# Attention of an encoder layer: scores three units ahead, a fourth slot of probabilities, one weighing run for a pair of units

## What is computed

```python
logits = jnp.einsum('bqkgd,bjkd->bkgqj', q_blk, k_blk) * scale + bias
logits = jnp.where(valid, logits, -jnp.inf)
m = jnp.maximum(jnp.max(logits, axis=-1), sink_f)
p = jnp.exp(logits - m[..., None])
denom = jnp.sum(p, axis=-1) + jnp.exp(sink_f - m)
probs = p / denom[..., None]
out = jnp.einsum('bkgqj,bjkd->bqkgd', probs, v_blk)
...
mix = jnp.concatenate([rms_norm(attn, g_attn), rms_norm(four, g_four)], axis=-1) @ w_o
x = layer_norm(ALPHA * x + mix, ln1_g, ln1_b)
```

## Time and profile before

| | |
|---|---|
| median of three runs (lowest, highest) | 962.12 us (962.06, 963.3) |
| the profiled execution: its own time, its span | 963.37 us, 961.6 us |
| busy, share of the span: TensorE, VectorE, ScalarE, GpSimd | 98%, 82%, 49%, 29% |
| attention stage in the trace | about 153 to 222 us |

### The profile page before, as it was taken

The page is one execution under the profiler, slowest core; times in us unless marked ns, Lnnn a source line. Parts: engine busy times, 40 slices in busy tenths (PEclk is TensorE's granted clock), DMA queues, the critical chain, the costliest instruction groups (busy, mean ns, idle before and its releaser), DMA issues.

```text
span 961.6 us, 12084 instructions
## 1 busy us (share of the span) xinstructions
PE 944.0 (98%) x4402; PEld 773.6 (80%) x4402; DVE 786.2 (82%) x1147; ACT 471.7 (49%) x706; POOL 282.2 (29%) x257
## 2 busy tenths in 40 slices
PE   7999999999999999999999999999999999999996
PEld 6888887667888788888888888888888888888885
DVE  5666488987886899889798888898888699977798
ACT  5575467868014664554455445445545754333200
POOL 2300327993940000010010001100000199990032
PEclk9999999999999999999999999999999999999999
DMA  8245153928031136365555464654527886564212
GB/s 312 83 87 175 22 132 136 304 45 305 10 144 43 67 91 160 79 164 132 121 142 134 100 172 100 142 148 105 153 66 262 339 340 232 190 229 171 96 66 109
DMA packets 110811, 142.06 MB, mean 148 GB/s; under 512 B 21164, under 2 KB 72320, under 8 KB 110753
## 3 DMA queue, kind: packets, MB, share of 16 engines
q1 hardware_dynamic: 104352, 129.69, 40.6%
q0 software_dynamic: 5184, 9.44, 7.2%
q10 hardware_dynamic: 1216, 2.17, 0.7%
HBM read 112.18 MB, written 47.97 MB: 167 GB/s over the span
## 4 chain that ended last, share of the span: by engine, by line
PE 93%; DVE 4%; issue 2%; DMA 1%; ACT 0%; POOL 0%; SPq 0%; DVEq 0%
PE ps L792 28%; PE ps L794 28%; PE ps L793 28%; PE ps L1042 2%; PE ps L1021 2%; DVE bn L1301 1%; DVE acc L1862 1%; PE ps L998 1%; PE ps L1154 1%; PE ps L999 1%; DMA acc<-in_x_prompt 1%; PE ps L827 1%; DVE pT L1518 0%; DVE prob L1510 0%; DVE mv L1305 0%
## 5 line engine op out<-in xcount | busy, mean ns | idle before, releaser
L792 PE MATMUL ps<-db_hi,ga_hi 128*128 128x512 f32 x252 | 98.0, 389 | 0.0
L793 PE MATMUL ps<-db_lo,ga_hi 128*128 128x512 f32 x252 | 98.0, 389 | 0.0
L794 PE MATMUL ps<-db_hi,ga_lo 128*128 128x512 f32 x252 | 98.0, 389 | 0.0
L792 PE MATMUL ps<-x1h,wa_hi 128*128 128x512 f32 x192 | 75.6, 394 | 0.0
L794 PE MATMUL ps<-x1h,w_lo 128*128 128x512 f32 x192 | 74.8, 389 | 0.0
L2220 ACT ACTIVATE hc<-U,taps 128x512 f32<-128x512 f32 x60 | 48.7, 813 | 53.1 <-DVE U L1697 41.5
L793 PE MATMUL ps<-x1l,wa_hi 128*128 128x512 f32 x192 | 74.7, 389 | 0.0
L737 POOL TENSOR_TENSOR acc<-acc,gain_bc 128x1024 f32<-128x1024 f32 x12 | 40.5, 3374 | 84.6 <-ACT bias_bc L1912 84.6
L2225 ACT ACTIVATE hc<-hc 128x512 f32<-128x512 f32 x44 | 27.9, 633 | 71.3 <-DVE hc L1714 71.3
L1912 ACT ACTIVATE ga_hi<-ga_raw 128x1536 fp32r<-128x1536 f32 x21 | 31.3, 1490 | 62.0 <-DMA db_raw<-in_w_down 28.8
L1298 DVE TENSOR_TENSOR ga_lo<-ga_raw,ga_hi 128x1536 fp32r<-128x1536 f32 x21 | 48.5, 2310 | 9.9 <-ACT ga_hi L1912 9.9
(11 more groups left out here) (314 smaller groups left out, 2892.5 us busy)
## 6 DMA issues: line engine op xcount, KB each, us to landing
w_raw<-in_w_up SPq DMA_DIRECT2D x44, 512.0 KB, 4.9
ga_raw<-gs_scratch SPq DMA_DIRECT2D x21, 768.0 KB, 4.6
ts_scratch<-in_w_down SPq DMA_DIRECT2D x12, 768.0 KB, 14.9
gs_scratch<-gsum SPq DMA_DIRECT2D x9, 1024.0 KB, 4.5
db_raw<-ts_scratch SPq DMA_DIRECT2D x12, 768.0 KB, 6.2
db_raw<-in_w_down SPq DMA_DIRECT2D x9, 768.0 KB, 6.5
ts_scratch<-in_w_down POOLq DMA_DIRECT2D x18, 256.0 KB, 5.1
gs_scratch<-gated SPq DMA_DIRECT2D x9, 512.0 KB
```

What stands on the lines that cost most here:

```text
L792: pe.matmul(out, whi, xhi, start=start, stop=False, skip_group_check=onto)
L793: pe.matmul(out, whi, xlo, start=False, stop=False, skip_group_check=onto)
L794: return pe.matmul(out, wlo, xhi, start=False, stop=stop, skip_group_check=onto)
```

## The change

A fourth slot of probabilities is added (`prob3`, for which the values of the second sequence move to another place), and `negm`, `rowsum` and `rden` get a fourth entry. TensorE's loop has a step more: step `m` has the scores of unit `m + 2` and the turns of unit `m - 1`. The weighing of a pair is one run of all key blocks, every second step. The second half of the last projection, `project(11, 1)`, stands among the scores of the first step, and the third run of `out_four` ahead of the last turns. On VectorE the two copies of a unit stand directly behind the four `logits`, and `attn_low` and `wo_low` behind them; ScalarE's loop follows the same steps. GpSimd's order stays, with four slots instead of three. No engine computes anything more or less.

```diff
-    negm = keep("negm", [P, 3, GRP])
+    negm = keep("negm", [P, 4, GRP])
...
-    vz1 = at("vz1", [P, TB, P], F32, 134912)
+    vz1 = at("vz1", [P, TB, P], F32, 184064)
...
     prob = at("prob", [P, 3, GRP, 3 * P + 1], F32, 8192)
+    prob3 = at("prob3", [P, GRP, 3 * P + 1], F32, 130816)
+    probs = [prob[:, 0], prob[:, 1], prob[:, 2], prob3[:]]
...
-            def weigh_pair(e, blocks):
+            def weigh_pair(e):
...
-                elif blocks[0] == 0:
+                else:
                     pe.wait_ge(o_sq, e - 1)
                     pe.wait_ge(o_lo, e - 1)
-                for i in blocks:
+                for i in range(len(kbs)):
...
-                if blocks[-1] == len(kbs) - 1:
-                    last.then_inc(pv_done, 1)
+                last.then_inc(pv_done, 1)
...
-            for n in range(UNITS):
-                if n == 1:
-                    project(11, 1)
-                if n >= UNITS - 2:
-                    out_four(n - UNITS + 2)
+            for m in range(UNITS + 1):
+                n = m - 1
+                if m >= UNITS - 2:
+                    out_four(m - UNITS + 2)
                 for j in range(GRP):
-                    if n + 2 < UNITS:
-                        scores(n + 2, j)
-                    if 1 <= j <= len(key_blocks(unit(n)[0])):
+                    if m + 2 < UNITS:
+                        scores(m + 2, j)
+                    if m == 0 and j == 2:
+                        project(11, 1)
+                    if m and 1 <= j <= len(key_blocks(unit(n)[0])):
                         turn_probs(n, j - 1)
-                if n >= 2:
-                    blocks = range(len(key_blocks(PAIRS[n // 2 - 1][0])))
-                    weigh_pair(n // 2 - 1, blocks[-1:] if n % 2 else blocks[:-1])
-            weigh_pair(UNITS // 2 - 1, range(2))
-            out_four(2)
+                if n >= 2 and n % 2 == 0:
+                    weigh_pair(n // 2 - 1)
+            weigh_pair(UNITS // 2 - 1)
             out_attn(0)
...
-                if n >= 3 and j == 0:
-                    dve.wait_ge(pt_ps, pt_before(n - 2))
+                if n >= 4 and j == 0:
+                    dve.wait_ge(pt_ps, pt_before(n - 3))
...
-            for n in range(UNITS):
-                for j in range(GRP):
-                    if n + 2 < UNITS and j < 2:
-                        logits(n + 2, j)
-                    if n == 1 and j == 1:
-                        proj_low(11)
-                    if n + 2 < UNITS and j == 1:
-                        logits(n + 2, 2)
-                        logits(n + 2, 3)
-                    if j == 1 and n >= 5 and n % 2:
-                        attn_low((n - 5) // 2)
-                    if j == 1 and n - 1 in WO_UNITS:
-                        wo_low(0, WO_UNITS.index(n - 1))
-                    if 1 <= j <= 2:
-                        probs_out(n, j - 1)
+            for m in range(UNITS + 1):
+                n = m - 1
+                if m + 2 < UNITS:
+                    for j in range(GRP):
+                        logits(m + 2, j)
+                if m == 0:
+                    proj_low(11)
+                    continue
+                for i in range(2):
+                    probs_out(n, i)
+                if n >= 5 and n % 2:
+                    attn_low((n - 5) // 2)
+                if m - 1 in WO_UNITS:
+                    wo_low(0, WO_UNITS.index(m - 1))
                 if n == UNITS - 1:
                     for k in range(4):
                         wo_low(1, k)
                     attn_low(UNITS // 2 - 2)
```

More of the change, by code:

```diff
@@ L210, in build @@
     nsink8 = keep("nsink8", [P, HEADS])
-    negm = keep("negm", [P, 3, GRP])
-    rowsum = keep("rowsum", [P, 3, GRP])
-    rden = keep("rden", [P, 3, GRP])
+    negm = keep("negm", [P, 4, GRP])
+    rowsum = keep("rowsum", [P, 4, GRP])
+    rden = keep("rden", [P, 4, GRP])
     vf = keep("vf", [P, TT])
@@ L699, in _ @@
             pool.wait_ge(s1_ps, NSEQ * FG)
-            for n in range(3):
+            for n in range(4):
                 set_sink(n)
@@ L706, in normalise @@
                 blk, b, kv = unit(n)
-                s = n % 3
+                s = n % 4
                 width = len(key_blocks(blk)) * P
@@ L712, in normalise @@
                 for j in range(GRP):
[L713 removed]
+                    pool.tensor_scalar(probs[s][:, j, 1:1 + width], probs[s][:, j, 1:1 + width], rden[:, s, j:j + 1], 1.0,
                                        ALU.mult, ALU.mult).then_inc(p_ready, 1)
[L715 to L716 removed]
+                if n + 4 < UNITS:
+                    set_sink(n + 4)
             def attn_squares(e):
@@ L1020, in turn_probs @@
                 for j in range(GRP):
-                    last = pe.transpose(ps[:, 3 + i, j * P:(j + 1) * P], prob[:, n % 3, j, 1 + i * P:1 + (i + 1) * P], ident[:])
+                    last = pe.transpose(ps[:, 3 + i, j * P:(j + 1) * P], probs[n % 4][:, j, 1 + i * P:1 + (i + 1) * P], ident[:])
                 last.then_inc(pt_ps, 1)
-            def weigh_pair(e, blocks):
+            def weigh_pair(e):
                 blk, b = PAIRS[e]
@@ L1506, in logits @@
                 h = kv * GRP + j
-                if n >= 3 and j == 0:
-                    dve.wait_ge(pt_ps, pt_before(n - 2))
+                if n >= 4 and j == 0:
+                    dve.wait_ge(pt_ps, pt_before(n - 3))
                 dve.wait_ge(s_ps, GRP * n + j + 1)
-                dve.tensor_tensor_reduce(prob[:, n % 3, j, 1:1 + width], ps[:, (GRP * n + j) % 3, 0:width],
+                dve.tensor_tensor_reduce(probs[n % 4][:, j, 1:1 + width], ps[:, (GRP * n + j) % 3, 0:width],
                                          bias8[:, h, first:first + width], -1.0, nsink8[:, h:h + 1],
-                                         ALU.add, ALU.min, negm[:, n % 3, j:j + 1]).then_inc(logit_done, 1)
+                                         ALU.add, ALU.min, negm[:, n % 4, j:j + 1]).then_inc(logit_done, 1)
             def probs_out(n, i):
@@ L2097, in exp @@
                     act.wait_ge(sink_set, n + 1)
-                act.activation(prob[:, n % 3, j, 0:1 + width], prob[:, n % 3, j, 0:1 + width], ACT.Exp, bias=negm[:, n % 3, j:j + 1], scale=-1.0,
-                               accum_out=rowsum[:, n % 3, j:j + 1]).then_inc(ex_done, 1)
+                act.activation(probs[n % 4][:, j, 0:1 + width], probs[n % 4][:, j, 0:1 + width], ACT.Exp, bias=negm[:, n % 4, j:j + 1], scale=-1.0,
+                               accum_out=rowsum[:, n % 4, j:j + 1]).then_inc(ex_done, 1)
             def probs_third(n):
@@ L2129, in _ @@
             exp(1, 3)
-            for n in range(UNITS):
-                if n == 1:
-                    proj_high(11)
+            for m in range(UNITS + 1):
+                n = m - 1
                 for j in range(GRP):
-                    if n + 2 < UNITS:
-                        exp(n + 2, j)
-                    if j == 2 and len(key_blocks(unit(n)[0])) == 3:
+                    if m + 2 < UNITS:
+                        exp(m + 2, j)
+                    if m == 0 and j == 2:
+                        proj_high(11)
+                    if m and j == 2 and len(key_blocks(unit(n)[0])) == 3:
                         probs_third(n)
@@ L2139, in _ @@
                     attn_high(n // 2 - 2)
-                if n in WO_UNITS:
-                    wo_high(0, WO_UNITS.index(n))
+                if m in WO_UNITS:
+                    wo_high(0, WO_UNITS.index(m))
                 elif n == UNITS - 1:
```

2 lines of the change are left out of this document (1 added, 1 removed).

## The result

The changed kernel takes 967.42 us (median of six, 966.37 to 967.83) where the kernel before takes 962.02 (six, 961.62 to 963.3): ratio 1.0047, 95% interval 1.0037 to 1.0058. It is slower: by 5.4 us in the medians, by 4.5 (3.6 to 5.6) in the ratio. The forecast was 967.3, 963.0 to 970.0.

A forecast was written before the change was run, and what follows sets the result against it. TensorE was taken to bound the attention stage, VectorE close behind. Merged runs (-2.2) and waits (+5.1) shift the last turns, then VectorE's list makes va +5.2: 962.12 + 5.2 = 967.3 us, range 963.0 to 970.0.

The forecast's parts named there:

- Part 1: TensorE up to the last turns: 13 weighing runs become 7, one pair of turns stands clear of scores; -2.2 us.
- Part 2: VectorE's new order with three score banks: TensorE waits 9.0 us in all against 3.9 before, +5.1 us.
- first kind: Steps 5, 7, 9, 11, 13: turns wait for the unit's first copy on VectorE, sum 2.8 us.
- second kind: Same five steps: the fourth score waits for its bank, freed by the late first logits, sum 2.6 us.
- steps 1 to 3: Start of attention: the last projection's low half ahead of unit 3's first logits delays scores and turns, sum 3.6 us.
- T15.0 comes at 224.9: First turn of unit 15: 218.24 before, plus 2.87 and 0.86 of work moved ahead, -2.2, +5.1.
- Weighing 7 ends at about 228.2 ... +3.4: End of attention, TensorE alone: last weighing, one run of 2.8, sums 1.7, giving 232.7 against 229.3.
- VectorE has a list in strict order ... and only then va ... +5.2: Behind the last turns, 9.7 us of VectorE work precedes va, which comes at 234.6 against 229.38.
- va released by VectorE's own wol1F: Sign at the end of attention: va follows VectorE's last weight low halves instead of waiting for TensorE.
- the first turn of the next stage: Follows va through the norm, 0.15 behind the norm's end; TensorE has no slack, so it ends +5.2 later.
- The contention of wol: Weight low halves on VectorE beside GpSimd: wol0A at 0.66 instead of 0.785 would make the end 0.5 us less late.
- rival of 0.04: TensorE's clock falls after more waits: half clock for 5 us of busy time, +2.5, 969.8 us; chance 0.04.

The follow-up runs named there:

- a_best_tail: Changed kernel with low halves in the steps ending in a weighing, first copy ahead of fourth logits, third output-projection run cut in two; 961.0 us, ratio 0.9984.
- b_run_early: Kernel before with only the third run of the Fourier half's output projection moved ahead of the last turns; 965.7 us, ratio 1.0026.
- a_best: a_best_tail with last projection's second half behind unit 2's last score, its low half behind unit 3's second logits; 962.0 us, ratio 0.9996.

## Why the prediction was right, and where not

- **Part 1, -2.2 for the merged runs.** Seven runs with 8 or 12 records, as said. The term was not measured alone, but the pair's length (9.31 against 9.28) contains it.
- **Part 2, waits of 9.0 us.** From start to start: first kind 2.81 (predicted 2.8), second kind 2.33 (2.6), steps 1 to 3 3.34 (3.6); 8.5 in all, in every step named. Undoing the second kind (with the wait for mal 5) and then the first gave 3.3 and 2.5 us. The mechanism is shown.
- **"T15.0 comes at 224.9".** 223.44, at +73.50, is 224.70 on the clock of before: 0.2 off.
- **"Weighing 7 ends at about 228.2 ... +3.4", TensorE alone.** This step failed. I gave the last weighing only the wait for the copy; it also waits for mal 5 (o_lo), two places behind it, 1.2 us more. The sums are 4.65 us late.
- **"VectorE has a list in strict order ... and only then va ... +5.2".** The list took 9.3 us instead of 9.7 (wol0A 0.66 each, the lower bound that I named) and began 0.2 earlier, so by itself it would have brought va at +4.60. The sums, made late by mal 5, released va instead, 0.16 later, at +4.76: the sign "va released by VectorE's own wol1F" did not come, by a hair. It came in the four kernels where va has no bracket. a_best_tail and b_run_early show the other side, va waiting 1.31 and 1.02 us for TensorE.
- **"the first turn of the next stage" follows va, and TensorE has no slack there.** Right but for some 0.2 us of slack: 46.42 behind va, as before, and 46.39 to 46.42 in every kernel but the one whose clock fell behind the sums. So the missed wait cost 0.16 us and not 1.2, because VectorE's list ended almost as late; that part is luck. The total was 0.4 us high at va (+5.2 for +4.76), mostly wol0A. Between medians the difference is 5.4, by ratio 4.5; the trace's 4.7 lies inside the interval.
- **The contention of wol.** Before, wol0A took 0.785 with GpSimd's squares beside it, which themselves took 1.25 instead of 0.75; after, GpSimd rests during wol0A, and it is 0.66. This is what the Trainium skill (GPSIMD Engine Reference, Key points) says of the shared interface; the trace agrees, and by my bound that was the lower end.
- **The clock.** Not the cause of the result in the profiled execution (granted 1.00 from 164 to 222), but no rival of 0.04 either: it halves in single executions of several of these kernels, for some 4 to 8 us, and cost 1.6 and 3.1 us in the two worked out here. The Trainium skill (TensorE: Matmul & The Clock Gate, A second HAM failure mode) tells that short idles between groups of matmuls can lower the clock; these two traces agree, while before's, with the same waits at the start of the stage, stayed at 1.00.

## What to carry to other kernels

Merging short runs into long ones saves a little on the engine that runs them and makes its demand uneven; then look at what stands ahead of each release on the other engine, since small instructions that nobody waits for (low halves here) now sit in the dense step. Put them in the step that has the long run, and the release ahead of what is not due yet. When you move an instruction, read every semaphore that its new neighbours wait on (o_lo here), and at the end of the stage work out every path to the next one, here TensorE's own work and the chain from va, since the later one sets the time and they can lie within 0.2 us. A busy share of 100% does not tell which: look at what the first instruction of the next stage follows at a constant distance over several kernels.

## What the hardware showed unexpectedly

- TensorE's granted clock fell to half behind 1.07 us of waiting and the one-column matmuls of the sums (b_run_early, 0.53 and 0.62), and behind waits of 0.85, 0.16 and 0.73 us in one profiled execution (0.57) but not in others with the same waits. Executions of the kernel before spread from 961.5 to 965.0 us, more than most terms here; how much of that is the clock is not shown.
- VectorE's wol and GpSimd's squares slow each other when they meet, by a fifth to four fifths: wol0A 0.785 from start to start for 0.66, the squares 1.25 for 0.75, wol0F rows up to 1.36 for 0.75. In a_best_tail wol0F kept its 0.74 and the squares beside it took 1.20; in a_best the squares kept 0.73 and wol0F took 1.22. Between these two traces GpSimd's squares moved from 0.13 us behind the start of wol0F to 0.06 ahead of it; what decides who loses is not shown further.
